# Router products made inside the second out stage instead of at the start of the route block

## The chip, the cores and the metric

The kernel runs on one core of a Trainium2 chip, as one program that is launched once. The metric is the device time of that launch in microseconds (us). The core has a matrix engine (TensorE, in the trace PE, with PEld for its weight loads), a vector engine (VectorE, DVE), a scalar engine (ScalarE, ACT), GpSimd (POOL), a sync engine that here only issues DMAs (SyncE, SP), and 16 DMA engines that all queues share. Each compute engine runs its own list of instructions in order, and they wait for each other by semaphores.

## The reference, cut to what matters

The network is two blocks for 512 tokens of width 1024. The first has two layers: a retention and gated-linear-attention mixer with a dense feed-forward part, then a gated mixer ("hgrn") with a mixture of experts. The second block has attention and a layer of many tiny experts. The change touches the seam between the second mixer and the mixture of experts:

```python
h = h + hgrn2_mixer(hn, lb, c_w_in[e], hgrn_norm_g[e], c_w_out[e])
h = h + moe_swiglu(rms_norm(h, norm_ffn_g[l]), moe_router[e], moe_w_gate[e], moe_w_up[e], moe_w_down[e])

def moe_swiglu(h, w_router, ...):
    logits = (xt @ w_router).astype(jnp.float32)        # 512 tokens x 8 experts
    top_logits, top_idx = lax.top_k(logits, TOP_K)      # TOP_K = 2
    gates = jax.nn.softmax(top_logits, axis=-1)
    ...                                                 # tokens sorted by expert, gate, up and down products
    out = jnp.einsum('nk,nkd->nd', gates.astype(y.dtype), y)
```

## The kernel before, in words

The 512 tokens are four tiles of 128 (`TT` = 4), the width is eight slices of 128 (`KD` = 8). `h` holds the running activations with tokens on partitions, `xT` the normalised input of the next product with the width on partitions. Both stay in SBUF. PSUM is eight banks, `ps[0]` to `ps[7]`.

The program is a row of blocks. A block gives each engine its list; all engines meet at its end, and nothing of the next block begins earlier. Within a block the order on each engine is as the code is written.

The second out stage (`out_stage` with the name "out1", L930) takes the mixer's output and, by token tile, scales heads, transposes (`turn`, L1058), multiplies by `c_w_out` (`project`, L1069), adds to `h` (`join`, L1026), normalises (ACT, L985 to L989, into `mix`), transposes the normalised rows (`turn_norm`, L1079) and writes them into `xT` with the gain (`place`, L1037). SP first loads `w_out`, then stores each normalised tile to `xn_rows` in DRAM, from which the experts gather later, and waits until the four stores have landed. The tail of the stage is tile 3: PE does the projection, `turn_norm(2)`, then `turn_norm(3)`, and DVE places.

The route block (`route_stage`, L1397) comes next. In it SP loads the router weights (32 KB); PE multiplies, in four tiles of eight slices (L1440), `xT` by them; DVE copies the four results (L1470), takes the two largest of eight (L1473, L1476) and marks them in `both`; PE counts, with ones and triangular matrices, how many tokens come before each in its expert (L1447, L1450); DVE works out from that the row of every token (L1495 to L1547). POOL, from the start of the block, sets a row of zeros and a 128x1024 tile of zeros (L1552, L1553), clears the table `token_of_row` (L1555), and when the rows are known scatters the token numbers into it with eight indirect DMAs (L1560). ACT, when the tile of zeros is set, issues one DMA that fills all of `y_rows`, 3072 rows of 4 KB, with zeros (L1457), later does one exponential (L1460), and at its end waits for the fill to land. POOL's last act is to wait for the scatters to land. A float32 product is two passes in the trace, so 32 products are 64 records.

The experts block starts with DVE's memset (L1812), POOL's fetch of indices (L1602) and SP's weight loads.

Of the kernel before, what the change touches and what calls it, by code (L numbers as in the profile page):

```python
# [14 lines left out]
F32 = mybir.dt.float32  # L15
# [7 lines left out]
P = 128  # L23
# [906 lines left out]

def out_stage(S, name, mix, gate, head_gain, w_sb, w, gain, scratch, ahead=None, xn_dram=None):
    nc, h, ps, xT = S.nc, S.h, S.ps, S.xT
    NH, ident = D // P, S.const("ident")
    squares, own, inverse, roots, ready, turned, taken = (
# [12 lines left out]
    with ExitStack() as st:  # L949
        ss = S.sb(name + "_ss", [P, TT, NH], F32, st)  # L950
        r = S.sb(name + "_r", [P, TT, NH], F32, st)
        hs = S.sb(name + "_hs", [P, TT], F32, st)
        hr = S.sb(name + "_hr", [P, TT], F32, st)
        with nc.Block(name) as block:
            @block.sync
            def _(sp):
                for c in range(2):
                    sp.dma_start(w_sb[:, c, :, :], w[:, c * 512:(c + 1) * 512].rearrange("(k p) n -> p k n", p=P)).then_inc(loaded[c].sem, 16)
                if ahead is not None:
                    ahead(sp)  # L960
                if xn_dram is not None:
                    for t in range(TT):
                        sp.wait_ge(h_normed.sem, h_normed.at(t + 1))
                        sp.dma_start(xn_dram[tile(t), :], mix[:, t, :]).then_inc(stored.sem, 16)
                    sp.wait_ge(stored.sem, stored.at(16 * TT))
# [36 lines left out]
            @block.vector  # L1002
            def _(dve):
                nonlocal n_own
                o = Count(own)
                ho = Count(h_own)

                def scale_heads(t):
                    m = mix[:, t, :].rearrange("p (h w) -> p h w", h=NH)
                    dve.wait_ge(squares.sem, squares.at(t + 1))  # L1010
                    nc.vector.tensor_reduce(ss[:, t, :], scratch[:, t % 2, :].rearrange("p (h w) -> p h w", h=NH), AX.X,
                                            ALU.add).then_inc(own.sem, o.up())
                    dve.wait_ge(own.sem, o.value())
                    nc.vector.tensor_scalar(ss[:, t, :], ss[:, t, :], 1.0 / P, EPS, ALU.mult, ALU.add).then_inc(own.sem, o.up())
                    dve.wait_ge(own.sem, o.value())
                    nc.vector.reciprocal(ss[:, t, :], ss[:, t, :]).then_inc(inverse.sem, 1)
                    nc.vector.tensor_tensor(mix[:, t, :], mix[:, t, :], gate[:, t, :], ALU.mult).then_inc(own.sem, o.up())
                    dve.wait_ge(own.sem, o.value())
                    dve.wait_ge(roots.sem, roots.at(t + 1))
                    nc.vector.tensor_tensor(m, m, r[:, t, :].unsqueeze(2).broadcast_to([P, NH, P]), ALU.mult).then_inc(ready.sem, 1)  # L1020

                def join(t):
                    for c in range(2):
                        dve.wait_ge(summed.sem, summed.at(2 * t + c + 1))
                        dst = h[:, t, c * 512:(c + 1) * 512]
# [14 lines left out]

                for t in range(TT):
                    scale_heads(t)
                for t in range(TT):
                    join(t)
                    invert(t)
                    if t:
                        place(t - 1)
                place(TT - 1)
                n_own = o.n

            @block.tensor
            def _(pe):
# [33 lines left out]
                for t in range(2, TT):  # L1086
                    turn(t)
                    turn_norm(t - 2)
                    project(t)
                turn_norm(TT - 2)  # L1090
                turn_norm(TT - 1)
        for sig, n in ((squares, TT), (own, n_own), (inverse, TT), (roots, TT), (ready, TT), (turned, TT), (taken, TT),
                       (h_squares, TT), (h_own, TT), (h_inverse, TT), (h_roots, TT), (h_normed, TT), (h_turned, 2 * TT),
                       (h_placed, 2 * TT), (stored, 16 * TT * (xn_dram is not None)), (loaded[0], 16), (loaded[1], 16),
                       (summed, 2 * TT), (joined, 2 * TT)):
            sig.base += n


def ffn_stage(S, M, mix, gate):
# [248 lines left out]
            s.base += n  # L1348


def mixer1(S, xn_rows):

    a = S.a
    w = a["c_w_in"][0]
    with ExitStack() as st:
# [3 lines left out]
        with ExitStack() as st2:  # L1359
# [9 lines left out]
            with ExitStack() as st3:  # L1369
# [5 lines left out]
            gated_stage(S, "hgrn", 8, 1, lambda p: q[:, p, :], lambda p: keys[:, p, :], lambda p: z[:, p, :],  # L1375
                        lambda hd, c: v[:, c, hd * P:(hd + 1) * P],
                        lambda hd: mix[:, :, hd * P:(hd + 1) * P], 0)
        w_out = S.sb("w_out1", [P, 2, KD, BANK], F32, st)
        scratch = S.sb("out1_squares", [P, 2, D], F32, st)
        out_stage(S, "out1", mix, gate, (S.head_gain["hgrn"], S.head_gain["hgrn"]), w_out, a["c_w_out"][0], S.gains[:, 3, :], scratch,  # L1380
                  xn_dram=xn_rows)


def scale_stage(S, x, by):
# [12 lines left out]
def route_stage(S, R):  # L1397
    nc, a, ps, xT = S.nc, S.a, S.ps, S.xT
    S_ = S.sig
    got, logits, own, gates_in, gates_e, chosen, placed, zeroed, ids, blanked = (  # L1400
        S_("o_" + x) for x in ("got", "logits", "own", "gates_in", "gates_e", "chosen", "placed", "zeroed", "ids", "blanked"))
    cleared, scattered = S_("o_cleared", pool_dma=True), S_("o_scattered", pool_dma=True)
    n_own = 0
    with ExitStack() as st:
        wr = S.sb("router_w", [P, KD, N_EXP], F32, st)
        lg = S.sb("router_lg", [P, TT, N_EXP], F32, st)
        top = S.sb("router_top", [P, TT, 8], F32, st)
        top_i = S.sb("router_ti", [P, TT, 8], U32, st)
        top_f = S.sb("router_tf", [P, TT, 8], F32, st)
# [17 lines left out]
        zero_rows = S.sb("router_zero", [1, LISTED], I32, st)  # L1427
        blank = S.sb("router_blank", [P, D], F32, st)
        with nc.Block("route") as block:
            @block.sync  # L1430
            def _(sp):
                with nc.allow_non_contiguous_dma(reason="32 KB of router weights"):
                    sp.dma_start(wr[:, :, :], a["moe_router"][0].rearrange("(k p) e -> p k e", p=P)).then_inc(got.sem, 16)

            @block.tensor
            def _(pe):
                pe.wait_ge(got.sem, got.at(16))
                for t in range(TT):
                    for k in range(KD):
                        last = nc.tensor.matmul(ps[t][:, 0:N_EXP], xT[:, k, t * P:(t + 1) * P], wr[:, k, :],  # L1440
                                                start=(k == 0), stop=(k == KD - 1))
                    last.then_inc(logits.sem, 1)

                pe.wait_ge(chosen.sem, chosen.at(1))
                for t in range(TT):
                    for u in range(t + 1):
# [17 lines left out]
            def _(dve):  # L1464
                nonlocal n_own
                o = Count(own)
                iota8 = S.const("iota16")[:, 0:8]
                for t in range(TT):
                    dve.wait_ge(logits.sem, logits.at(t + 1))
                    nc.vector.tensor_copy(lg[:, t, :], ps[t][:, 0:N_EXP]).then_inc(own.sem, o.up())  # L1470
                dve.wait_ge(own.sem, o.value())
                for t in range(TT):
                    nc.vector.max(top[:, t, :], lg[:, t, :]).then_inc(own.sem, o.up())  # L1473
                dve.wait_ge(own.sem, o.value())
# [76 lines left out]
            def _(pool):  # L1551
# [9 lines left out]
                            out=R.token_of_row, out_offset=bass.IndirectOffsetOnAxis(ap=R.row[:, t, c:c + 1], axis=0),  # L1561
                            in_=token_i[:, t:t + 1], in_offset=None).then_inc(scattered.sem, 16)
                pool.wait_ge(scattered.sem, scattered.at(16 * 2 * TT))
        for s, n in ((got, 16), (logits, TT), (own, n_own), (gates_in, 1), (gates_e, 1), (chosen, 1), (placed, 1),
                     (zeroed, 2), (cleared, 16), (blanked, 16), (scattered, 32 * TT), (ids, 2)):
            s.base += n

# [295 lines left out]
    return eng.value_load(tile, min_val=lo, max_val=hi)  # L1863


def moe1(S, xn_rows):

    nc, a = S.nc, S.a
    with ExitStack() as st:
# [2 lines left out]
        R.row = S.sb("row_of", [P, TT, 2], I32, st)  # L1872
        R.expert = S.sb("expert_of", [P, 2, 16], I32, st)
        R.units = S.sb("n_units", [P, 2], I32, st)
        R.xn = xn_rows
        R.y = nc.dram_tensor("y_rows", (ROWS_MAX, D), F32, kind="Internal").ap()
        R.token_of_row = nc.dram_tensor("token_of_row", (LISTED, 1), I32, kind="Internal").ap()
        route_stage(S, R)
# [1311 lines left out]
def run_stages(S, out):  # L3190
# [6 lines left out]
    M = modulation(S, S.stack)  # L3197
    xn_rows = S.nc.dram_tensor("xn_rows", (T, D), F32, kind="Internal").ap()
    mixer0(S, M)
    mixer1(S, xn_rows)  # L3200
    for prefix in ("t_", "h_", "q_", "s_", "m_"):
        S.retire(prefix)
    moe1(S, xn_rows)
    row_norm_stage(S, "final1", S.a["final_norm_g"])
    with ExitStack() as st:
        mix = S.sb("mix2", [P, TT, D], F32, st)
# [53 lines left out]
```

## Time and profile before

| what | value |
|---|---|
| time, median of 3 runs | 4557.43 us (4549.16, 4557.43, 4559.23) |
| time of the profiled execution | 4559.06 us |
| span of its trace | 4557.0 us, 2.06 us less than its time |
| PE busy | 3855.7 us, 85% of the span |
| DVE, ACT, POOL busy | 1715.8, 585.3, 1099.9 us |
| mean granted clock of TensorE | 0.907 of full |
| out stage of the second mixer | 1285.8 to 1366.5 us |
| route block | 1366.5 to 1411.8 us |

Times in the trace are microseconds from the start of the span. The chain that ended last, as the page prints it, covers less than one per cent of the span, since the chain breaks at the ends of blocks; so the seam is read from the timeline, from the waits and from the DMA rows.

### The profile page before, as it was taken

Reading aid. Unit: us, or ns where it says so; the run is one execution under the profiler, and the core shown is the slowest. Engines: PE = TensorE matmul, PEld = TensorE weight load, DVE = VectorE, ACT = ScalarE, POOL = GpSimd, SP = SyncE. Lnnn points to the kernel's source line nnn. Section 1 sums busy time; section 2 is a strip of 40 time slices with the busy share of each in tenths; the row PEclk is TensorE's granted clock in tenths of the full one; section 3 lists DMA queues with packets and bytes.
Section 4 is the critical chain, followed back from the end, with each engine's and each line's share of the span. In section 5 each row is a group of like instructions: output and inputs, shape, how many; then the busy total and the mean of one; then the engine's idle time right before and its main releaser. Section 6 shows DMA issues by size and latency. Waiting matters only on the chain. (4 is left out here: it accounts for less than half of the span.)

```text
span 4557.0 us, 45375 instructions
## 1 busy us (share of the span) xinstructions
PE 3855.7 (85%) x17173; PEld 2566.8 (56%) x17180; DVE 1715.8 (38%) x3657; ACT 585.3 (13%) x1486; POOL 1099.9 (24%) x1165
## 2 busy tenths in 40 slices
PE   7988999999676999999999986998666777676666
PEld 3465777644645888888999983465322223222222
DVE  2042231111941000000000004184988776777655
ACT  1121000112320000000000001143111111111111
POOL 0010000000411000000000000000477777777775
PEclk9969999999897999999999998979788888888888
DMA  3103674320017888888777752102799999999998
GB/s 117 56 2 132 235 264 162 138 74 19 1 56 286 298 301 303 307 304 298 257 260 249 259 197 67 54 1 80 298 406 404 420 417 412 420 416 415 418 415 337
DMA packets 531782, 1088.29 MB, mean 239 GB/s; under 512 B 36993, under 2 KB 315934, under 8 KB 531526
## 3 DMA queue, kind: packets, MB, share of 16 engines
q1 hardware_dynamic: 376330, 522.81, 33.5%
q0 software_dynamic: 150976, 546.79, 29.8%
q10 hardware_dynamic: 4348, 17.07, 0.9%
q8 instruction: 69, 1.13, 0.1%
q14 instruction: 59, 0.48, 0.0%
HBM read 1065.29 MB, written 21.28 MB: 238 GB/s over the span
## 5 line engine op out<-in xcount | busy, mean ns | idle before, releaser
L2634 PE MATMUL banks<-peer_ring,mix 128*128 128x512 f32 x1512 | 843.2, 718 | 359.6 <-DMA peer_ring<-in_peer_v_dram,peer_expert 359.6
L2634 PEld LDWEIGHTS banks<-peer_ring,mix 128*128 128x128 f32 x1512 | 337.8, 231 | 861.3 <-DMA peer_ring<-in_peer_v_dram,peer_expert 452.2
L2902 DVE SCALAR_TENSOR_TENSOR peer_ring<-peer_ring,banks 128x1024 f32<-128x1024 f32 x512 | 593.6, 1217 | 250.1 <-DMA peer_ring<-in_peer_u_dram,peer_expert 249.1
L2502 POOL DMA_INDIRECT peer_ring<-in_peer_u_dram,peer_expert x512 | 481.3, 940 | 658.8 <-DVE peer_expert L2836 456.2
L2502 POOL DMA_INDIRECT peer_ring<-in_peer_v_dram,peer_expert x512 | 488.1, 953 | 162.1 <-issue 143.7
L1809 DVE TENSOR_TENSOR experts_hid<-experts_gs,banks 128x128 f32<-128x128 f32 (+1 forms) x224 | 66.5, 297 | 1169.4 <-ACT experts_gs L1781 1169.4
L1690 PEld LDWEIGHTS banks<-rows_xt,experts_wg 128*128 128x128 f32 x3584 | 447.6, 192 | 36.9 <-issue 36.6
L1690 PE MATMUL banks<-rows_xt,experts_wg 128*128 128x128 f32 (+1 forms) x3584 | 463.1, 283 | 3.2 <-DVE rows_xt L1629 3.2
L1690 PE MATMUL banks<-rows_xt,experts_wu 128*128 128x128 f32 (+1 forms) x3584 | 461.8, 282 | 0.0
L1690 PEld LDWEIGHTS banks<-rows_xt,experts_wu 128*128 128x128 f32 x3584 | 441.8, 192 | 0.0
L402 PE MATMUL banks<-xT,proj_w 128*128 128x512 f32 (+2 forms) x736 | 328.1, 604 | 8.7 <-PEq L216 7.1
L1602 POOL DMA_DIRECT2D rows_index<-token_of_row x14 | 8.0, 574 | 1070.6 <-PE banks L1618 1063.1
L405 PE MATMUL banks<-proj_w,xT 128*128 128x512 f32 (+2 forms) x704 | 265.6, 536 | 0.0
L854 POOL TENSOR_TENSOR hgrn_both<-k,hgrn_diff 128x256 f32<-128x256 f32 x56 | 50.6, 910 | 836.5 <-ACT hgrn_diff L799 810.5
L1707 PE MATMUL banks<-experts_wd,experts_hid 128*128 128x512 f32 x560 | 251.9, 592 | 0.0
L402 PEld LDWEIGHTS banks<-xT,proj_w 128*128 128x128 f32 (+2 forms) x736 | 138.0, 189 | 192.2 <-issue 191.4
L1781 ACT ACTIVATE experts_gs<-banks 128x128 f32<-128x128 f32 (+1 forms) x224 | 63.8, 285 | 1174.1 <-PE banks L1690 1174.1
L405 PEld LDWEIGHTS banks<-proj_w,xT 128*128 128x128 f32 x704 | 126.9, 195 | 140.6 <-issue 140.4
L2935 DVE SCALAR_TENSOR_TENSOR banks<-peer_ring,peer_wgt,banks 128x1024 f32<-128x1024 f32 x130 | 167.4, 1288 | 84.6 <-DMA peer_ring<-in_peer_v_dram,peer_expert 83.9
L1720 PE MATMUL banks<-experts_hid,experts_wd 128*128 128x152 f32 x1344 | 180.5, 293 | 0.0
L1720 PEld LDWEIGHTS banks<-experts_hid,experts_wd 128*128 128x128 f32 x1344 | 176.3, 190 | 0.4
L1173 PE MATMUL banks<-xT,ffn_wg 128*128 128x256 f32 x704 | 162.1, 384 | 1.2 <-ACT ada_c L1211 1.2
(449 smaller groups left out, 3635.1 us busy)
## 6 DMA issues: line engine op xcount, KB each, us to landing
experts_wg<-in_moe_w_gate_dram SPq DMA_DIRECT2D x112, 1024.0 KB, 5.1
experts_wu<-in_moe_w_up_dram SPq DMA_DIRECT2D x112, 1024.0 KB, 7.7
experts_wd<-in_moe_w_down_dram SPq DMA_DIRECT2D x112, 1024.0 KB, 8.1
ada_w<-in_w_ada_dram SPq DMA_DIRECT2D x12, 2048.0 KB, 8.0
ffn_wg<-in_ffn_w_gate_dram SPq DMA_DIRECT2D x22, 1024.0 KB, 7.9
ffn_wu<-in_ffn_w_up_dram SPq DMA_DIRECT2D x22, 1024.0 KB, 10.4
ffn_wd<-in_ffn_w_down_dram SPq DMA_DIRECT2D x22, 1024.0 KB, 11.9
proj_w<-in_c_w_in_dram SPq DMA_DIRECT2D x8, 2048.0 KB, 8.5
```

What stands on the lines that cost most here:

```text
L402: last = nc.tensor.matmul(out_of(g), wk[:, m * P:m * P + width], xT[:, k, :], start=(k == 0), stop=(k == KD - 1))
L405: last = nc.tensor.matmul(out_of(g), xT[:, k, m * P:(m + 1) * P], wk[:, 0:n], start=(k == 0), stop=(k == KD - 1))
L1173: last = nc.tensor.matmul(ps[bank][:, 0:ROWS], w[:, b, k, j * P:(j + 1) * P], xT[:, k, u * ROWS:(u + 1) * ROWS], start=(k == 0), stop=(k = ...
L1690: ins = nc.tensor.matmul(ps[bank][:, 0:E.rows], w[:, b, k, j * P:(j + 1) * P], E.xu[:, k, :], start=(k == 0), stop=(k == KD - 1))
L1707: ins = nc.tensor.matmul(ps[hf][:, :], hid[:, j, 0:P], wd[:, b, j, hf * 512:(hf + 1) * 512], start=(first and j == 0), stop=(final and j = ...
L1720: ins = nc.tensor.matmul(ps[d // 2][:, at:at + B.rows], wd[:, b, j, d * P:(d + 1) * P], hid[:, j, :], start=False, stop=False, skip_group_ ...
L1781: nc.scalar.activation(gs[:, j, 0:E.rows], ps[4 + j][:, 0:E.rows], ACT.Silu).then_inc(E.gated[j].sem, 1)
L1809: nc.vector.tensor_tensor(hid[:, j, 0:E.rows], gs[:, j, 0:E.rows], ps[6 + j][:, 0:E.rows], ALU.mult).then_inc(E.hidden[j].sem, 1)
L2502: pool.indirect_dma_start(out=ring[:, slot_of(kind, n, b), :], out_offset=None, in_=tables[kind == "value"], in_offset=bass.IndirectOffset ...
L2634: last = nc.tensor.matmul(ps[bank + hf][:, :], diag[:, n % 2 * B + b, :], ring[:, slot_of("value", n, b), hf * 512:(hf + 1) * 512], start= ...
L2902: nc.vector.scalar_tensor_tensor(row, row, 1.0, rows_at, ALU.mult, ALU.mult, accum_out=acts[:, t % 2, at:at + 1]).then_inc(dotted[q].sem, 1)
L2935: ins = nc.vector.scalar_tensor_tensor(sum_at, row, weight(n, b), sum_at, ALU.mult, ALU.add)
```

## The change

The router weights are loaded by SP in the out stage, after `w_out` and ahead of the stores. PE makes the products there: `route(0)` and `route(1)` between the transposes of tile 2 and those of tile 3, `route(2)` and `route(3)` after them, all into one bank, `ps[0]`, 8 columns a tile. DVE copies the 128x32 result once, after its last `place`, into a tile `router_logits` that lives to the end of the program. The route block loses its SP list, its 32 products and four copies. The semaphores with the prefix `t_` are given free a little earlier, so that the new signals find two.

```diff
+                if logits_to is not None:
+                    with nc.allow_non_contiguous_dma(reason="32 KB of router weights"):
+                        sp.dma_start(router[:, :, :], S.a["moe_router"][0].rearrange("(k p) e -> p k e", p=P)).then_inc(router_got.sem, 16)
                 if xn_dram is not None:
...
                 place(TT - 1)
+                if logits_to is not None:
+                    dve.wait_ge(logits.sem, logits.at(TT))
+                    nc.vector.tensor_copy(logits_to, ps[0][:, 0:TT * N_EXP].rearrange("p (t e) -> p t e", t=TT)).then_inc(own.sem, o.up())
...
+                def route(t):
+                    if logits_to is None:
+                        return
+                    pe.wait_ge(h_placed.sem, h_placed.at(2 * t + 2))
+                    if t == 0:
+                        pe.wait_ge(router_got.sem, router_got.at(16))
+                    for k in range(KD):
+                        last = nc.tensor.matmul(ps[0][:, t * N_EXP:(t + 1) * N_EXP], xT[:, k, tile(t)], router[:, k, :],
+                                                start=(k == 0), stop=(k == KD - 1))
+                    last.then_inc(logits.sem, 1)
+
                 turn_norm(TT - 2)
+                route(0)
+                route(1)
                 turn_norm(TT - 1)
+                route(2)
+                route(3)
...
-            @block.sync
-            def _(sp):
-                with nc.allow_non_contiguous_dma(reason="32 KB of router weights"):
-                    sp.dma_start(wr[:, :, :], a["moe_router"][0].rearrange("(k p) e -> p k e", p=P)).then_inc(got.sem, 16)
-
             @block.tensor
             def _(pe):
-                pe.wait_ge(got.sem, got.at(16))
-                for t in range(TT):
-                    for k in range(KD):
-                        last = nc.tensor.matmul(ps[t][:, 0:N_EXP], xT[:, k, t * P:(t + 1) * P], wr[:, k, :],
-                                                start=(k == 0), stop=(k == KD - 1))
-                    last.then_inc(logits.sem, 1)
-
                 pe.wait_ge(chosen.sem, chosen.at(1))
...
-                for t in range(TT):
-                    dve.wait_ge(logits.sem, logits.at(t + 1))
-                    nc.vector.tensor_copy(lg[:, t, :], ps[t][:, 0:N_EXP]).then_inc(own.sem, o.up())
-                dve.wait_ge(own.sem, o.value())
```

The list of PE at the seam, before: the last projection, both transposes together, the end of the out stage, and the route block with the products and the two counts.

```order
L1069 MATMUL banks<-w_out,xT 128x512 x16
L1079 MATMUL banks<-consts,mix 128x128 x16
L954 UNCONDITIONAL_BRANCH
L1435 UNCONDITIONAL_BRANCH
L1440 MATMUL banks<-router_w,xT 128x8 x32
L1447 MATMUL banks<-router_both,consts 128x8 x10
L1450 MATMUL banks<-router_both,consts 128x8 x4
```

The same place in the changed kernel (its line numbers are higher by 9 to 15):

```order
L1078 MATMUL banks<-w_out,xT 128x512 x16
L1088 MATMUL banks<-consts,mix 128x128 x8
L1106 MATMUL banks<-router_w,xT 128x8 x16
L1088 MATMUL banks<-consts,mix 128x128 x8
L1106 MATMUL banks<-router_w,xT 128x8 x16
L957 UNCONDITIONAL_BRANCH
L1457 UNCONDITIONAL_BRANCH
L1462 MATMUL banks<-router_both,consts 128x8 x10
L1465 MATMUL banks<-router_both,consts 128x8 x4
```

Half of the products now stand ahead of the last transposes, half behind them, and all ahead of the branch that ends the out stage; the counts are the first thing that PE does in the route block. On DVE, before, the four copies open the route block:

```order
L1037 TENSOR_TENSOR xT<-banks,columns 128x4x128 x4
L954 UNCONDITIONAL_BRANCH
L1463 UNCONDITIONAL_BRANCH
L1470 COPY router_lg<-banks 128x8 x4
L1473 MAX router_top<-router_lg 128x8 x4
```

and in the changed kernel one copy closes the out stage:

```order
L1043 TENSOR_TENSOR xT<-banks,columns 128x4x128 x4
L1057 COPY router_logits<-banks 128x32
L957 UNCONDITIONAL_BRANCH
L1478 UNCONDITIONAL_BRANCH
L1484 MAX router_top<-router_logits 128x8 x4
```

The choice of experts is now the first thing that DVE does in the route block. ACT's and POOL's lists at the seam are the same in both.

## Rows read from the trace of the kernel before

**Rows 1.** Page, first line: the span.

```profile
span 4557.0 us, 45375 instructions
```

**Rows 2.** Timeline, tail of out1: start us, us, engine, line, operation, count, idle before.

```profile
1334.83 8.75 PE L1069 MATMUL banks<-w_out,xT 128*128 128x512 f32 x20
...
1359.64 1.04 PE L1079 MATMUL banks<-consts,mix 128*128 128x128 f32 x8
...
1363.57 1.09 PE L1079 MATMUL banks<-consts,mix 128*128 128x128 f32 x8 [2.89 <-ACT mix L989]
1364.26 1.29 DVE L1037 TENSOR_TENSOR xT<-banks,columns 128x512 f32<-128x512 f32 x2 [0.98 <-PE banks L1079]
```

**Rows 3.** Waits of SP's queue, 1340 to 1430: us in total, times, longest.

```profile
SPq L1429 <- PEq L1429: 44.6, 1, 44.6
...
SPq L954 <- DMA xn_rows<-mix: 2.3, 1, 2.3
```

**Rows 4.** Timeline of the route block, 1366 to 1414.

```profile
1366.55 0.39 SPq L1433 DMA_DIRECT2D router_w<-in_moe_router_dram  x1
1366.56 2.86 POOL L1552 MEMSET router_zero<- 1x3328 int32 x1 [86.93 <-POOLq L954]
...
1368.77 13.82 PE L1440 MATMUL banks<-router_w,xT 128*128 128x8 f32 x64 [4.11 <-DMA router_w<-in_moe_router_dram]
1369.36 0.94 POOL L1553 MEMSET router_blank<- 128x1024 f32 x1
1370.34 0.45 ACTq L1457 DMA_DIRECT2D y_rows<-router_blank  x1
1370.62 0.72 POOL L1555 DMA_DIRECT2D token_of_row<-router_zero  x1 [0.31 <-POOL router_blank L1553]
...
1382.63 0.17 DVE L1470 COPY router_lg<-banks 128x8 f32<-128x8 f32 x1 [3.25 <-PE banks L1440]
1382.84 0.37 DVE L1473 MAX8 router_top<-router_lg 128x8 f32<-128x8 f32 x4
...
1384.71 4.43 PE L1447 MATMUL banks<-router_both,consts 128*128 128x8 f32 x20 [2.11 <-DVE router_both L1485]
...
1395.16 0.16 DVE L1534 CAST router_token<-consts 128x4 int32<-128x4 f32 x1
...
1396.24 1.07 POOL L1560 DMA_INDIRECT token_of_row<-router_token,row_of  x1 [24.90 <-DVE router_token L1534]
...
1405.19 0.95 POOL L1560 DMA_INDIRECT token_of_row<-router_token,row_of  x1 [0.31 <-issue]
1411.85 0.27 DVE L1812 MEMSET experts_zero<- 128x256 uint32 x1 [15.09 <-PEq L1429]
```

**Rows 5.** DMA issues, 1340 to 1440: KB each, median us from issue to landing.

```profile
y_rows<-router_blank ACTq DMA_DIRECT2D x1, 12288.0 KB, 39.2
...
token_of_row<-router_token,row_of POOLq DMA_INDIRECT x8, 6.4
...
token_of_row<-router_zero POOLq DMA_DIRECT2D x1, 13.0 KB, 7.8
```

**Rows 6.** Windows, DMA in the route block: us, busy by engine, PEclk, DMA share, GB/s.

```profile
1375.40:1376.50 1.10, 1.10 (x7) 1.10 (x7) 0.17 (x1) 0.00 (x0) 0.00 (x0) 0.50 1.05 403
1376.50:1380.00 3.50, 3.50 (x18) 3.50 (x18) 0.17 (x1) 0.00 (x0) 0.00 (x0) 0.50 1.02 415
1380.00:1396.20 16.20, 8.74 (x41) 8.55 (x40) 7.04 (x54) 0.20 (x1) 0.00 (x0) 0.50 1.02 421
1396.20:1401.20 5.00, 0.00 (x0) 0.00 (x0) 0.48 (x4) 0.00 (x0) 3.95 (x4) 0.50 1.02 422
1401.20:1402.70 1.50, 0.00 (x0) 0.00 (x0) 0.00 (x0) 0.00 (x0) 0.99 (x2) 0.50 0.30 56
1402.70:1411.50 8.80, 0.00 (x0) 0.00 (x0) 0.00 (x0) 0.00 (x0) 2.83 (x3) 0.50 0.03 2
```

**Rows 7.** Windows at the seam, for the granted clock (PEclk).

```profile
1363.50:1364.70 1.20, 1.09 (x8) 0.85 (x8) 0.44 (x1) 0.01 (x1) 0.00 (x0) 1.00 0.32 126
1364.70:1368.70 4.00, 0.00 (x0) 0.00 (x0) 0.85 (x2) 0.00 (x0) 2.14 (x1) 0.52 0.37 101
```

**Rows 8.** Windows at a stretch of 128x1 products in the first block.

```profile
882.40:886.90 4.50, 4.50 (x42) 4.46 (x40) 0.76 (x2) 0.00 (x0) 0.00 (x0) 1.00 0.00 0
887.00:891.90 4.90, 4.90 (x24) 4.86 (x23) 0.00 (x0) 0.00 (x0) 0.00 (x0) 0.50 0.02 3
```

**Rows 9.** Timeline, the change of blocks from hgrn to out1.

```profile
1284.94 0.60 ACT L812 ACTIVATE mix<-banks 128x512 f32<-128x512 f32 x1 [7.62 <-PE banks L911]
1285.79 0.99 SPq L958 DMA_DIRECT2D w_out<-in_c_w_out_dram  x2
```

More of the change, by code:

```diff
@@ L929, in gated_stage, with out_stage @@
             s.base += n
-def out_stage(S, name, mix, gate, head_gain, w_sb, w, gain, scratch, ahead=None, xn_dram=None):
+def out_stage(S, name, mix, gate, head_gain, w_sb, w, gain, scratch, ahead=None, xn_dram=None, logits_to=None):
     nc, h, ps, xT = S.nc, S.h, S.ps, S.xT
@@ L953, in out_stage @@
         hr = S.sb(name + "_hr", [P, TT], F32, st)
+        if logits_to is not None:
+            router = S.sb("router_w", [P, KD, N_EXP], F32, st)
+            router_got, logits = S.sig("o_got"), S.sig("o_logits")
         with nc.Block(name) as block:
@@ L1048, in _ @@
                 place(TT - 1)
+                if logits_to is not None:
+                    dve.wait_ge(logits.sem, logits.at(TT))
+                    nc.vector.tensor_copy(logits_to, ps[0][:, 0:TT * N_EXP].rearrange("p (t e) -> p t e", t=TT)).then_inc(own.sem, o.up())
                 n_own = o.n
@@ L1096, in out_stage @@
             sig.base += n
+        if logits_to is not None:
+            router_got.base += 16
+            logits.base += TT
 def ffn_stage(S, M, mix, gate):
@@ L1348, in close, with mixer1 @@
             s.base += n
-def mixer1(S, xn_rows):
+def mixer1(S, xn_rows, logits):
     a = S.a
@@ L1377, in mixer1 @@
                         lambda hd: mix[:, :, hd * P:(hd + 1) * P], 0)
+        S.retire("t_")
         w_out = S.sb("w_out1", [P, 2, KD, BANK], F32, st)
@@ L1380, in mixer1 @@
         out_stage(S, "out1", mix, gate, (S.head_gain["hgrn"], S.head_gain["hgrn"]), w_out, a["c_w_out"][0], S.gains[:, 3, :], scratch,
-                  xn_dram=xn_rows)
+                  xn_dram=xn_rows, logits_to=logits[:, :, :])
 def scale_stage(S, x, by):
@@ L1399, in route_stage @@
     S_ = S.sig
-    got, logits, own, gates_in, gates_e, chosen, placed, zeroed, ids, blanked = (
-        S_("o_" + x) for x in ("got", "logits", "own", "gates_in", "gates_e", "chosen", "placed", "zeroed", "ids", "blanked"))
+    own, gates_in, gates_e, chosen, placed, zeroed, ids, blanked = (
+        S_("o_" + x) for x in ("own", "gates_in", "gates_e", "chosen", "placed", "zeroed", "ids", "blanked"))
     cleared, scattered = S_("o_cleared", pool_dma=True), S_("o_scattered", pool_dma=True)
@@ L1404, in route_stage @@
     with ExitStack() as st:
-        wr = S.sb("router_w", [P, KD, N_EXP], F32, st)
-        lg = S.sb("router_lg", [P, TT, N_EXP], F32, st)
+        lg = R.logits
         top = S.sb("router_top", [P, TT, 8], F32, st)
@@ L1563, in _ @@
                 pool.wait_ge(scattered.sem, scattered.at(16 * 2 * TT))
-        for s, n in ((got, 16), (logits, TT), (own, n_own), (gates_in, 1), (gates_e, 1), (chosen, 1), (placed, 1),
+        for s, n in ((own, n_own), (gates_in, 1), (gates_e, 1), (chosen, 1), (placed, 1),
                      (zeroed, 2), (cleared, 16), (blanked, 16), (scattered, 32 * TT), (ids, 2)):
@@ L1863, in expert_values, with moe1 @@
     return eng.value_load(tile, min_val=lo, max_val=hi)
-def moe1(S, xn_rows):
+def moe1(S, xn_rows, logits):
     nc, a = S.nc, S.a
@@ L1874, in moe1 @@
         R.units = S.sb("n_units", [P, 2], I32, st)
-        R.xn = xn_rows
+        R.xn, R.logits = xn_rows, logits
         R.y = nc.dram_tensor("y_rows", (ROWS_MAX, D), F32, kind="Internal").ap()
@@ L3199, in run_stages @@
     mixer0(S, M)
-    mixer1(S, xn_rows)
+    logits = S.sb("router_logits", [P, TT, N_EXP])
+    mixer1(S, xn_rows, logits)
     for prefix in ("t_", "h_", "q_", "s_", "m_"):
         S.retire(prefix)
-    moe1(S, xn_rows)
+    moe1(S, xn_rows, logits)
     row_norm_stage(S, "final1", S.a["final_norm_g"])
```

## The prediction, written before the changed kernel ran

> **What bounds the kernel now.** I took the span first [rows 1]: the profiled execution took 4559.06 us, of which 4557.0 are the span and 2.06 lie around it. The change lies in some 50 us of that, so shares of the whole span say nothing; I read the timeline of the seam, then who waits for whom at the ends of the two blocks, then the DMA rows.
>
> In the route block the reader is to see two chains side by side, and that all engines meet at its end: SP, with nothing to do after one DMA, waits 44.6 us for that [rows 3]. The block runs from 1366.55 to 1411.85, 45.3 us [rows 4]. Chain one is the obvious one: weights land, 64 passes of L1440 (13.82 us), the last copy at 1382.63, MAX8 at 1382.84, counts on PE at 1384.71, rows known at 1395.16, eight scatters issued from 1396.24 to 1405.19, the last of them landing. With the median landing of 6.4 us [rows 5] that is 1405.19 + 6.4 = 1411.6, 0.25 before the next block: this chain ends the block now. Chain two starts at the block's start too and uses none of these engines but POOL for two memsets: the tile of zeros, then at 1370.34 the fill of `y_rows`, 12288 KB, landing 39.2 us later, at 1409.5 [rows 4, 5]. It ends only 2.1 us before chain one. The DMA engines are full with it (421 GB/s, share 1.02) until 1401.2 [rows 6]; 12.58 MB at 421 GB/s is 29.9 us, so it can't be much shorter. From 1401.2 to 1409.5 there is a tail in which only some 0.1 MB moves (56 GB/s for 1.5 us, then 2), while the last scatters are issued.
>
> **The change, part by part.** Everything is counted against the profiled execution.
>
> *What goes.* DVE's MAX8 stood 1382.84 - 1366.55 = 16.3 us into the block. It will stand some 0.1 us into it, so chain one moves forward by 16.2 us against the block's start: the first scatter 29.7 - 16.2 = 13.5 us in, the last 38.6 - 16.2 = 22.4 us in, landed at 22.4 + 6.4 = 28.8 us. The one thing that could hold the first scatter is the clearing of the table, issued 4.07 us in and landed 7.8 later, at 11.9 [rows 4, 5]: 1.6 us to spare. ACT's exponential can't come before POOL's memsets and the fill's issue are through, at 4.2 us, but DVE then waits for the counts (until 8 us) anyway.
>
> *What is late next.* The fill. Its start hangs on the memsets at the block's start, which don't move within the block: DMA full until 34.65 us in (1401.2), the small remainder until 36.15 (1402.7) [rows 6]. That is later than 28.8, so from here on chain two decides. What the tail does then is what no row shows. Below: it goes with the scatters that are gone by then, and the block ends at 34.65 + 0.3 = 35.0. Above: it stays as it is, 1409.5 is 42.95 us in, plus 0.3, 43.3. I take the nearer row, the end of the remainder, 36.15. On top come the eight scatters, which now run beside the fill. The nearest row is the clearing: while its packets pass, 403 instead of 421 GB/s for 1.1 us, and 415 in the 3.5 us after [rows 6], 0.05 and 0.05 us; eight such are 0.8 us. From landing to the next block's first instruction 0.3 (at another change of blocks ACT ends at 1285.54 and SP issues at 1285.79 [rows 9]), and 0.4 for the last packet to land. Block: 36.15 + 0.8 + 0.4 + 0.3 = 37.65 instead of 45.3, a gain of 7.65 us. More than half of the 16.2 is thus not to be had.
>
> *What comes.* PE's tail of the out stage [rows 2]. `turn_norm(2)` ends at 1360.68 and PE waits for ACT until 1363.57, 2.89 us. `route(0)` and `route(1)` are 32 passes there. A pass with few columns costs at full clock what 128x1 passes cost: 42 in 4.50 us, 0.107 [rows 8]; 32 are 3.42 us, to 1364.10, so `turn_norm(3)` is 0.53 late and ends at 1365.2. Then `route(2)` and `route(3)`, 32 passes, for which the clock decides. It is granted at 1.00 (2.4 GHz) until about 1364.8, then 0.50 (1.2 GHz) [rows 7]. Before it fell PE had done one burst of eight transposes after 2.89 us of nothing. The new passes fill the time, but passes of few columns did not keep or win the clock in this trace: it fell at 886.9 in the middle of an unbroken run of them [rows 8], and 13.82 us of L1440 ran at 0.50 to the end [rows 4, 6]. So I price them at half clock: 13.82/64 = 0.216 each, 6.9 us, to 1372.1. If the clock stayed, they'd cost 3.4; if it fell before `route(0)`, the first 32 would cost 3.4 more and the transposes 0.9 more. The copy adds 0.1 wait and 0.2: 1372.4. `place(3)` is through by 1366.5 and is hidden. Before, the stage ended with SP's wait for the last store [rows 3] at about 1366.2; that store doesn't move and is now hidden too. With 0.25 for the change of blocks the route block starts at 1372.65 instead of 1366.55: 6.1 us later. All that the block holds, the fill first, starts later by that. The 32 KB of weights come behind 4 MB of `w_out`, some 60 us before they are wanted, and SP's first store comes 30 us later: no cost.
>
> **The sum.** +6.1 - 7.65 = -1.55 us. All that follows shifts as a whole. By bounds: best +2.7 (full clock) - 10.3 = -7.6; worst +10.4 (clock lost early) - 2.0 = +8.4. The profiled execution lies 1.6 above the median of the runs, so a run like it would take 4557.5, and 4556 to 4557 is what I expect of a median; I say 4556.5.
>
> **Rivals.** *A, the fill is held up by the scatters in its midst (the other side: slower).* Between 1402.7 and 1409.5 the rest of the fill crept, in the very stretch where POOL issued one scatter every 1.27 us. If an engine gives the fill a packet only as each scatter passes, then eight scatters inside the fill hold such an engine for 8 x 1.27 = 10.2 us, and the block ends at 36.15 + 10.2 + 0.7 = 47.05: +1.75 and +6.1, +7.9 us in all, 4566. It decides from 7.65 - 6.1 = 1.55 us of hold-up. Against it: four scatters were issued from 1396.2 to 1401.2 and the rate stayed at 422 GB/s [rows 6], and the clearing cost little. The Trainium skill ("DMA: Bandwidth & Descriptors", section on latency and other measured facts) calls two of the 16 engines usually slower, with contention by GpSimd's descriptor rings as a guess; by that the tail belongs to one or two engines and stays whole, which is the upper bound of 43.3 above, +4.1 us in all. No row splits the engines. Chance 0.2 for A and this weaker form together.
>
> *B, the scatters don't get through until the fill has.* The first was issued at 1396.24 and the fill filled the engines until 1401.2; with 6.4 us to landing it landed after the fill's end. If they queue, all eight land in a burst behind 34.65 us, in 6.4 us at least and 10.4 (1401.2 to 1411.6) at most: block 41.4 to 45.4, taken 42.5, so +3.3 us, 4561. Against it: the clearing, issued at 1370.62 into the same load, landed in 7.8 us [rows 5], long before the fill's end. The same page (section on queues, rings and completion order) says that a DMA engine takes turns between its queues; by that rule B is out, and the clearing's row agrees. Chance 0.12.
>
> *C, the fill doesn't bound the block, and the chain's 16.2 us count in full.* 6.1 - 16.2 = -10.1, 4548. For it: nothing but the tail's obscurity; 12.58 MB would have to go at over 500 GB/s. Chance 0.05.
>
> *D, the clock stays at 1.00 through `route(2)` and `route(3)`.* 3.5 us less than forecast, -5.0, 4553. For it: PE is never idle now from 1334 to the end of the stage. Against: rows 8. Chance 0.08.
>
> **How the numbers follow.** Forecast 0.55, A 0.2, B 0.12, C 0.05, D 0.08. What a measurement can tell from no change is 0.2%, about 9 us; the three runs shown alone lie 10 us apart. The forecast, B and D are inside it wholly, A nearly (+7.9), C just outside. With the runs' own scatter: faster 0.1, same 0.8, slower 0.1. The range goes from 4549 (C's edge and the lowest run) to 4564 (most of A).
>
> **What would show it.** PE's L1106 in two groups of 32 records, the second near 0.21 us a record; the first in the hole before the last transposes; route block starting near 1372.7; MAX8 at once; first scatter some 13.5 us after its start; the block 37 to 38 us long, and its end at the landing of the fill, not of the scatters. It is wrong if the block is under 33 us (C) or over 41 (A, B), or the second group runs at 0.107 (D). A change elsewhere in the trace of more than a few us would be a cause that I haven't seen.

## The result, and the profile after

The changed kernel is slower: 1.0074 times the kernel before, 95% interval 1.0061 to 1.0086, medians 4591.65 us (five runs) and 4559.23 us (seven). Measured again beside the kernel before (run e1_after) it was 1.0088 (1.0071 to 1.0105), medians 4596.55 and 4557.19. Forecast was 4556.5, no change. Two more runs of the changed kernel were disturbed (6398 us at a mean granted clock of 0.587, and 17699 us) and are left out, and the trace read here is that of e1_after.

```profile
span 4588.3 us, 45433 instructions
```

The span is 31.3 us above the one before [rows 1]. The first look goes to the seam. From the timeline of e1_after, the tail of out1, in the form of [rows 2]; L1088 is `turn_norm`, L1106 the router products, L1043 `place`, L1057 the new copy:

```profile
1349.99 1.04 PE L1088 MATMUL banks<-consts,mix 128*128 128x128 f32 x8
1350.86 3.64 PE L1106 MATMUL banks<-router_w,xT 128*128 128x8 f32 x32
...
1354.36 1.38 PE L1088 MATMUL banks<-consts,mix 128*128 128x128 f32 x8
1355.03 1.44 DVE L1043 TENSOR_TENSOR xT<-banks,columns 128x512 f32<-128x512 f32 x2 [1.39 <-PE banks L1088]
1355.53 6.83 PE L1106 MATMUL banks<-router_w,xT 128*128 128x8 f32 x32
1362.40 0.19 DVE L1057 COPY router_logits<-banks 128x32 f32<-128x32 f32 x1 [5.94 <-PE banks L1106]
1362.88 2.86 POOL L1563 MEMSET router_zero<- 1x3328 int32 x1 [92.66 <-POOLq L957]
```

The first 32 passes take 3.64 us and lie in the old hole, the second 32 take 6.83, the copy follows at once. The granted clock in the same three stretches (PEclk is the third value from the end):

```profile
1349.90:1354.30 4.40, 4.40 (x41) 4.31 (x40) 2.19 (x5) 2.50 (x4) 0.00 (x0) 1.00 0.00 0
1354.30:1355.50 1.20, 1.20 (x10) 1.20 (x10) 0.47 (x1) 0.00 (x0) 0.00 (x0) 0.78 0.67 266
1355.50:1362.40 6.90, 6.87 (x34) 6.77 (x32) 0.91 (x2) 0.00 (x0) 0.00 (x0) 0.50 0.09 32
```

PE was busy throughout, and the clock still fell to 0.50 (1.2 GHz) at about 1355, as in [rows 7, 8]. From the transposes of tile 2 to POOL's first memset it is 12.89 us now, 6.92 before (1359.64 to 1366.56): +5.97.

The route block, in the form of [rows 4]:

```profile
1362.91 0.37 DVE L1484 MAX8 router_top<-router_logits 128x8 f32<-128x8 f32 x4 [0.32 <-PEq L957]
...
1364.00 1.78 DVE L1490 CAST router_tf<-router_ti 128x32 f32<-128x32 uint32 x1
...
1366.69 0.45 ACTq L1472 DMA_DIRECT2D y_rows<-router_blank  x1
...
1377.92 1.07 POOL L1571 DMA_INDIRECT token_of_row<-router_token,row_of  x1 [10.22 <-DVE router_token L1545]
...
1386.88 0.96 POOL L1571 DMA_INDIRECT token_of_row<-router_token,row_of  x1 [0.30 <-issue]
1411.64 0.27 DVE L1823 MEMSET experts_zero<- 128x256 uint32 x1 [33.21 <-PEq L1456]
```

MAX8, the choice of the experts, comes at once, the eight scatters are issued from 15.0 to 24.0 us into the block, and then there are 24 us in which no compute engine does anything. The block is 48.76 us long, 3.5 us longer than the 45.29 of before. Its DMA issues, in the form of [rows 5], and the DMA in windows, in the form of [rows 6]:

```profile
y_rows<-router_blank ACTq DMA_DIRECT2D x1, 12288.0 KB, 44.4
token_of_row<-router_token,row_of POOLq DMA_INDIRECT x8, 13.0
```

```profile
1368.00:1383.50 15.50, 4.53 (x22) 4.43 (x21) 5.73 (x39) 0.67 (x2) 4.36 (x5) 0.50 1.02 420
1383.50:1388.00 4.50, 0.00 (x0) 0.00 (x0) 0.00 (x0) 0.00 (x0) 3.42 (x4) 0.50 1.19 249
1388.00:1398.00 10.00, 0.00 (x0) 0.00 (x0) 0.00 (x0) 0.00 (x0) 0.00 (x0) 0.50 1.03 167
1398.00:1402.50 4.50, 0.00 (x0) 0.00 (x0) 0.00 (x0) 0.00 (x0) 0.00 (x0) 0.50 1.09 88
1402.50:1410.00 7.50, 0.00 (x0) 0.00 (x0) 0.00 (x0) 0.00 (x0) 0.00 (x0) 0.50 0.91 367
```

The DMA rate is 420 GB/s, falls to 249, 167 and 88 GB/s while the DMA engines stay fully busy (share 1.03 to 1.19; it can exceed 1, since the times of packets are added up), and recovers as the last scatter lands (issued at 1386.88, landed 16.8 us later, at 1403.7). The queues in the slow stretch, 1383.5 to 1402.5: packets, MB, and the time of their packets as a share of the 16 engines' time; q10 is the fill, q0 the scatters:

```profile
q10 hardware_dynamic: 777, 3.18, 105.1%
q0 software_dynamic: 256, 0.00, 2.9%
```

In the full stretch before it, 1368 to 1383.5, q10 has

```profile
q10 hardware_dynamic: 1585, 6.49, 101.9%
```

So the scatters hardly take time of the engines themselves. A packet of the fill takes 16 x 15.5 x 1.019 / 1585 = 0.16 us in the full stretch and 16 x 19 x 1.051 / 777 = 0.41 us beside the scatters, on average. The fill lands 44.4 us after its issue, at 1411.1, and the next block begins 0.5 later. So the seam costs 5.97 + 3.47 = +9.4 us. That leaves most of the loss to be found elsewhere, and the forecast had nothing elsewhere.

It is in the last block, whose 1024 gathers (L2513, L2502 before) bring table rows of 4 KB into `peer_ring`. `peer_ring` is their ring of buffers. For that tile the trace answers with first and last issue (behind the durations in ns); before, then e1_after:

```profile
L2502 POOL DMA_INDIRECT peer_ring<-in_peer_u_dram,peer_expert x512: 933/937/1421, 3189.1 to 4487.4; - x171
L2502 POOL DMA_INDIRECT peer_ring<-in_peer_v_dram,peer_expert x512: 932/937/1919, 3313.7 to 4522.3; - x171
```

```profile
L2513 POOL DMA_INDIRECT peer_ring<-in_peer_u_dram,peer_expert x512: 932/937/1810, 3192.8 to 4517.2; - x171
L2513 POOL DMA_INDIRECT peer_ring<-in_peer_v_dram,peer_expert x512: 932/937/1935, 3317.4 to 4552.6; - x171
```

3189.1 to 4522.3 is 1333.2 us, 3192.8 to 4552.6 is 1359.8: +26.6. A window of 1000 us in this stage, before and in e1_after:

```profile
3500.00:4500.00 1000.00, 701.71 (x1301) 282.59 (x1302) 698.92 (x1367) 115.20 (x378) 751.94 (x796) 0.85 1.02 417
```

```profile
3500.00:4500.00 1000.00, 696.93 (x1272) 281.47 (x1273) 684.74 (x1344) 113.02 (x371) 733.22 (x777) 0.84 1.02 407
```

417 against 407 GB/s with the DMA share at 1.02 in both: the stage is bound by DMA, and the same engines, equally busy, move 2.4% less. The gathers' queue in this window, before and in e1_after:

```profile
q0 software_dynamic: 114384, 416.52, 102.3%
```

```profile
q0 software_dynamic: 111720, 406.81, 102.3%
```

Fewer packets in the same engine time: each takes 2.4% longer. What reads the ring is not slower (median of L2902, now L2913, on VectorE 1217 ns in both, of the products on PE 592 ns in both). No instruction of this stage was changed. What was changed is where its tiles lie: `router_logits`, 128 bytes on each partition, is allocated for the rest of the program, and all tiles allocated after it begin 128 bytes higher. `peer_ring` went from address 153088 (a multiple of 256, and of 512) to 153216 (128 above one), as the allocations add up.

The two parts are 9.4 + 26.6 = 36.0 us; the ratios, at 4557 us, say 33.7 (27.8 to 39.2) and 40.1 (32.4 to 47.8). The spans of the two traces differ by 31.3 only. The rest is in stretches that the change leaves alone and that differ from one execution to the next: up to `turn_norm(2)` e1_after took 9.65 us less than before (in e2_pad128 below, where nothing before the seam differs in its instructions either, the fill was issued 9.2 us earlier), and between the combination of the experts' results and the first gather into `peer_ring` 4.8 us more. So single traces are compared here stage by stage, and the whole by the ratios.

### The profile page after: what moved, and what is told of

Its sections match the earlier page's. It is cut to its first block and busy times, and to the rows that moved or that the text cites. A ratio compares the mean times of both kernels' runs of the same rounds, so it can differ in the third digit from the quotient of the medians.

```text
span 6396.5 us, 45433 instructions
## 1 busy us (share of the span) xinstructions
PE 5914.2 (92%) x17173; PEld 3431.9 (54%) x17180; DVE 1715.0 (27%) x3654; ACT 585.7 (9%) x1486; POOL 1097.7 (17%) x1165
## 5 line engine op out<-in xcount | busy, mean ns | idle before, releaser
L2645 PE MATMUL banks<-peer_ring,mix 128*128 128x512 f32 x1512 | 1068.6, 885 | 182.1 <-DMA peer_ring<-in_peer_v_dram,peer_expert 182.1
L1701 PEld LDWEIGHTS banks<-rows_xt,experts_wg 128*128 128x128 f32 x3584 | 707.1, 260 | 86.1 <-issue 77.7
L1701 PE MATMUL banks<-rows_xt,experts_wg 128*128 128x128 f32 (+1 forms) x3584 | 738.9, 387 | 2.4 <-DVE rows_xt L1640 2.4
L1701 PE MATMUL banks<-rows_xt,experts_wu 128*128 128x128 f32 (+1 forms) x3584 | 738.6, 387 | 0.0
L1701 PEld LDWEIGHTS banks<-rows_xt,experts_wu 128*128 128x128 f32 x3584 | 705.8, 269 | 6.6
L2913 DVE SCALAR_TENSOR_TENSOR peer_ring<-peer_ring,banks 128x1024 f32<-128x1024 f32 x512 | 593.7, 1218 | 263.6 <-DMA peer_ring<-in_peer_u_dram,peer_expert 262.7
L2513 POOL DMA_INDIRECT peer_ring<-in_peer_u_dram,peer_expert x512 | 483.1, 943 | 804.2 <-DVE peer_expert L2847 570.6
L402 PE MATMUL banks<-xT,proj_w 128*128 128x512 f32 (+2 forms) x736 | 542.9, 926 | 7.6 <-PEq L216 6.6
L2513 POOL DMA_INDIRECT peer_ring<-in_peer_v_dram,peer_expert x512 | 491.2, 959 | 193.8 <-issue 127.3
L405 PE MATMUL banks<-proj_w,xT 128*128 128x512 f32 (+2 forms) x704 | 460.6, 842 | 0.0
L1718 PE MATMUL banks<-experts_wd,experts_hid 128*128 128x512 f32 x560 | 444.1, 966 | 0.0
L1200 PE MATMUL banks<-xT,ffn_wu 128*128 128x256 f32 x704 | 279.3, 583 | 0.0
L1210 PE MATMUL banks<-ffn_wd,ffn_hid 128*128 128x512 f32 x352 | 274.9, 967 | 0.0
```

The lines of the kernel that those rows point to most:

```text
L402: last = nc.tensor.matmul(out_of(g), wk[:, m * P:m * P + width], xT[:, k, :], start=(k == 0), stop=(k == KD - 1))
L405: last = nc.tensor.matmul(out_of(g), xT[:, k, m * P:(m + 1) * P], wk[:, 0:n], start=(k == 0), stop=(k == KD - 1))
L1200: last = nc.tensor.matmul(ps[bank][:, 0:ROWS], w[:, b, k, j * P:(j + 1) * P], xT[:, k, u * ROWS:(u + 1) * ROWS], start=(k == 0), stop=(k = ...
L1210: last = nc.tensor.matmul(ps[2 * s + half][:, :], hid[:, j, s * P:(s + 1) * P], wd[:, b, j, half * 512:(half + 1) * 512], start=(g == 0 an ...
L1701: ins = nc.tensor.matmul(ps[bank][:, 0:E.rows], w[:, b, k, j * P:(j + 1) * P], E.xu[:, k, :], start=(k == 0), stop=(k == KD - 1))
L1718: ins = nc.tensor.matmul(ps[hf][:, :], hid[:, j, 0:P], wd[:, b, j, hf * 512:(hf + 1) * 512], start=(first and j == 0), stop=(final and j = ...
```

## The experiments

**The changed kernel again, and the kernel before with its tiles moved.** e1_after is the changed kernel.

> The changed kernel again, for a trace at the usual clock and for its time beside the kernel before. Theory 1 (placement): the new tile router_logits, 128 bytes a partition, lives to the end of the program and moves every later tile by 128 bytes, so that the ring into which the last block gathers its table rows (peer_ring) no longer begins on a multiple of 256 bytes; then the route block is at most 5 us off the forecast, and the 1240 us of gathers take some 30 us longer (about 410 GB/s instead of 420), whole +30 to +37 us. Theory 2 (seam): the scatters hold up the fill or the clock is lost at the seam; then the surplus of some 33 us stands between 1360 us and the experts' first product, and the gathers run at 420 GB/s. Theory 3 (experts): their weight loads are slower, surplus between 1430 and 2720 us.

Measured: 1.0088, with the trace above. Theory 1 holds for the larger part and theory 2 for a smaller one: the gathers took 26.6 us longer, and the route block was not within 5 us of the forecast, as theory 1 alone would have it, but 11 us longer (48.76 against 37.65). The experts' stage, from its first memset to the first gather of the combination, took 1310.6 us against 1311.4, so theory 3 falls.

e2_pad128 is the kernel before with one more line:

```diff
+    S.sb("unused", [P, TT, N_EXP])
     mixer1(S, xn_rows)
```

> The kernel before with nothing but an unused tile of 128 bytes a partition allocated where the changed kernel has router_logits; no instruction differs but in SBUF addresses. Theory 1 (placement): +30 to +35 us, in the gathers of the last block. Theories 2 and 3 as far as they need the moved instructions: within 0.1% of the kernel before.

Measured: 1.0053 (1.0037 to 1.0070), +24 us. Its gathers:

```profile
L2502 POOL DMA_INDIRECT peer_ring<-in_peer_u_dram,peer_expert x512: 932/937/1813, 3179.7 to 4503.5; - x171
L2502 POOL DMA_INDIRECT peer_ring<-in_peer_v_dram,peer_expert x512: 932/937/1937, 3304.4 to 4540.1; - x171
```

1360.4 us. An unused tile of 128 bytes, with every instruction of before, brings the whole +27 in the gathers. The whole is less than the +30 to +35 expected.

**The changed kernel with its tiles put back.** e3_after_512:

```diff
-    logits = S.sb("router_logits", [P, TT, N_EXP])
+    logits = S.sb("router_logits", [P, 4 * TT, N_EXP])[:, 0:TT, :]
```

> The changed kernel with router_logits allocated four times as large (512 bytes a partition, of which the first 128 are used), so that every later tile moves by 512 bytes in all and keeps its place modulo 512. Theory 1 (placement): the surplus goes, and what is left is the seam's own effect, -2 us by the forecast, within -8 to +8. Theory 2: stays at +30 us.

Measured: 1.0014 (1.0004 to 1.0024), +6.4 us. The gathers go from 3196.7 to 4530.9, 1334.2 us, as before. What is left is the seam: route block from 1369.78 to 1418.80, 49.0 us, fill landing after 44.6. By the ratio it is +1.8 to +10.9 us, by the trace +9.4.

e4_after_ring:

```diff
+        S.sb("peer_gap", [P, 96], F32, st)
         ring = S.sb("peer_ring", [P, 2 * B, D], F32, st)
```

> The changed kernel with an unused tile of 384 bytes a partition just ahead of peer_ring, so that the ring and what lies behind it in the last stage are back on their place modulo 512, and the experts' and the attention's tiles stay moved by 128. Theory 1, if the ring alone is it: the whole surplus of 30 us goes, as in the run with the 512-byte tile. If the experts' weight loads have a share (theory 3): that share stays.

Measured: 1.0014 (1.0005 to 1.0024), gathers 1333.7 us. The same as with all tiles put back, so moving the experts' and the attention's tiles by 128 bytes cost nothing to be seen. That is no test of alignment in those stages: by the allocations their large tiles lay off a multiple of 256 before as well (the experts' first weight tile at 76992, 192 above one, and now at 77120, 64 above one). What aligning them would give, no run shows.

**Which tile and which step.** Four kernels are the kernel before with unused bytes ahead of and behind `peer_ring` (e8_behind128 has none ahead and 128 behind):

```diff
+        S.sb("gap_ahead", [P, 16], F32, st)          # 16, 32 or 64 words: 64, 128 or 256 bytes
         ring = S.sb("peer_ring", [P, 2 * B, D], F32, st)
+        S.sb("gap_behind", [P, 112], F32, st)        # so that both make 512
```

> The kernel before with unused tiles of 64 bytes ahead of peer_ring and 448 behind it: the ring alone moves by 64 bytes, its neighbours by 512. If it is the ring's place modulo 256 that sets the gathers' rate: gathers 1333 -> about 1360 us, +25 us in all. If only a shift by 128 hurts, or another tile is the cause: no change.

> The kernel before with the ring alone moved by 128 bytes (128 ahead, 384 behind). Theory 1, the ring's place: +25 us, as in the run in which all tiles moved by 128 (+24). If another tile of the last stage than the ring is the cause: no change.

> The kernel before with the ring alone moved by 256 bytes (256 ahead, 256 behind). If a multiple of 256 is what counts: within 0.1% of the kernel before. If a multiple of 512 is needed, or any shift against the neighbours costs: +12 to +25 us.

> The kernel before with 128 unused bytes behind peer_ring: the ring stays, the weights, sums and keys behind it move by 128. Theory 1: no change, within 0.1%. If VectorE's operands behind the ring are the cause: +25 us.

| ring moved by | behind it moved by | ratio (95%) | gathers, first to last issue | 3500 to 4500 |
|---|---|---|---|---|
| 64 bytes | 512 | 1.0064 (1.0047 to 1.0080) | 3189.5 to 4550.4, 1360.9 us | 407 GB/s |
| 128 | 512 | 1.0063 (1.0045 to 1.0081) | 3179.9 to 4541.1, 1361.2 us | 407 GB/s |
| 256 | 512 | 0.9998 (0.9989 to 1.0008) | 3185.5 to 4517.6, 1332.1 us | 417 GB/s |
| 0 | 128 | 1.0004 (0.9994 to 1.0014) | 3188.7 to 4522.2, 1333.5 us | 417 GB/s |

It is the ring alone, and a multiple of 256 bytes is enough. 64 and 128 bytes off cost the same within the intervals. The windows of e5_ring64 and e7_ring256:

```profile
3500.00:4500.00 1000.00, 685.82 (x1272) 278.09 (x1274) 685.84 (x1345) 113.21 (x371) 732.86 (x777) 0.84 1.02 407
```

```profile
3500.00:4500.00 1000.00, 707.75 (x1308) 285.14 (x1310) 698.00 (x1366) 116.09 (x385) 752.28 (x796) 0.85 1.02 417
```

The Trainium skill ("DMA: Bandwidth & Descriptors", section on how a descriptor splits into AXI transactions) says that an aligned descriptor goes out in pieces of 256 bytes, and that a read which starts off such a boundary also moves the bytes below it. It speaks of reads; here the side that was moved is the one written, in SBUF. The step at 256 agrees with it. By its count of pieces, an estimate, a row of 4096 bytes goes from 16 to 17 for either shift, 6%, and by its count of bytes a shift of 128 costs twice one of 64; the runs show 2.4% less for both. So the size of the loss comes out of neither count. That extra pieces are the cause is argued; that the address is, is shown.

**What the scatters do to the fill.** e9_after_wait, on top of e3_after_512:

```diff
                 pool.wait_ge(ids.sem, ids.at(2))
+                pool.wait_ge(blanked.sem, blanked.at(16))
                 for t in range(TT):
```

> The changed kernel with router_logits at 512 bytes, and POOL waits for the fill of y_rows to land before it issues the first scatter. If the scatters slow the fill (rival A in another form): the fill goes at 420 GB/s to its end and lands some 33 us after its issue instead of 44.4; then come the eight scatters alone, some 10 us of issuing and 3 to 5 to land, block about 51 us. If the fill is slow for another reason (more bytes, its later start, DMA engines busy otherwise): it still lands after 44 us.

Measured: 1.0025 (1.0015 to 1.0034). Its issues and windows:

```profile
y_rows<-router_blank ACTq DMA_DIRECT2D x1, 12288.0 KB, 32.8
token_of_row<-router_token,row_of POOLq DMA_INDIRECT x8, 3.8
```

```profile
1374.00:1383.50 9.50, 3.95 (x19) 3.85 (x19) 5.41 (x37) 0.11 (x1) 0.00 (x0) 0.50 1.02 405
1383.50:1402.50 19.00, 0.00 (x0) 0.00 (x0) 0.34 (x3) 0.00 (x0) 0.00 (x0) 0.50 1.02 410
```

Without scatters beside it the fill keeps above 400 GB/s and lands after 32.8 us; the scatters then land in 3.8 instead of 13.0 (medians). The block, 1368.30 to 1420.73, is 52.4 us, since one follows the other.

e10_after_half, on top of e3_after_512, has `for t in range(TT // 2)` around the scatters, so that only the tokens of tiles 0 and 1 reach the table; the scatters of the others are left out.

> The changed kernel with router_logits at 512 bytes and only the four scatters of token tiles 0 and 1; those of tiles 2 and 3 are left out, so that the experts work on other rows. If each scatter takes its share from the fill: the fill lands about 38.5 us after its issue, midway between 33 and 44.4, and the route block is some 6 us shorter than with eight. If it is the mere presence of scatters, or something else in the block: still 44.

Measured in one execution: the fill lands after

```profile
y_rows<-router_blank ACTq DMA_DIRECT2D x1, 12288.0 KB, 37.9
```

and the block, 1362.33 to 1404.61, is 42.3 us. So 0, 4 and 8 scatters give 32.8, 37.9 and 44.6 us: 1.3 and 1.7 us for each. Each scatter carries 128 numbers of 4 bytes, 512 bytes in all, next to nothing at 420 GB/s. That the scatters lengthen the fill is shown by this row of three; why a packet of the fill takes longer beside them is not.

**The fill out of the way.** e11_after_early, on top of e3_after_512: POOL sets the zeros in the out stage, SP issues the fill there, and the route block has none.

```diff
+                if fill is not None:
+                    sp.wait_ge(zeroed.sem, zeroed.at(1))
+                    sp.dma_start(fill.rearrange("(a p) d -> p a d", p=P),
+                                 blank[:, :].unsqueeze(1).broadcast_to([P, ROWS_MAX // P, D])).then_inc(blanked.sem, 16)
                 if xn_dram is not None:
...
-                act.dma_start(R.y.rearrange("(a p) d -> p a d", p=P),
-                              blank[:, :].unsqueeze(1).broadcast_to([P, ROWS_MAX // P, D])).then_inc(blanked.sem, 16)
```

> The changed kernel with router_logits at 512 bytes, the tile of zeros set by POOL and the fill issued by SP in the out stage, behind the weights there. The fill (30 us) is over by 1335. Then the route block is chain one alone: first scatter 13 to 15 us in, last issued at 24, landed by 29; 29 to 31 us instead of 48.8, and the whole 17 to 19 us below the run with the 512-byte tile, 8 to 12 us below the kernel before. If chain one is slow by itself when it starts early: 35 us or more.

Measured: 0.9982 (0.9971 to 0.9992), median 4545.0 us, 8 us below the kernel before by the ratio (4 to 13). From the load of `w_out` to the route block it is 86.5 us, as in e3_after_512, so the early fill costs the out stage nothing. The route block of e11_after_early, its first memset, first scatter, last scatter, and on DVE the start of the next block:

```profile
1362.62 2.87 POOL L1575 MEMSET router_zero<- 1x3328 int32 x1 [85.54 <-POOLq L960]
...
1377.69 1.07 POOL L1582 DMA_INDIRECT token_of_row<-router_token,row_of  x1 [11.17 <-DVE router_token L1557]
...
1386.64 0.95 POOL L1582 DMA_INDIRECT token_of_row<-router_token,row_of  x1 [0.30 <-issue]
1392.87 0.27 DVE L1834 MEMSET experts_zero<- 128x256 uint32 x1 [14.66 <-PEq L1472]
```

The block is 30.25 us long, as forecast for chain one alone (29 to 31). e12_before_early does the same to the kernel before.

> The kernel before with the same early fill and the products still in the route block (semaphores with the prefix t_ are given free before the out stage, as in the changed kernel). Chain one decided there already: the block shortens only by the quicker landing of the last scatters, some 2 to 3 us, 4555 us. Against it the early fill of the changed kernel shows what moving the products is worth once the fill is out of the way: -16.2 + 6.1, about -10 us.

Measured: 0.9998 (0.9987 to 1.0009); block from 1354.77 to 1399.68, 44.9 us, only 0.4 shorter where 2 to 3 had been expected, since chain one ends it: the last scatter landed 4.9 us after its issue here and 5.3 before (median of all eight before: 6.4), so there was little to win. In both, 1.35 us lie between that landing and the next block. Between the two, the products moved are worth 44.91 - 30.25 = 14.7 us in the block, less 6.0 in the out stage: 8.7, and by the ratios 0.9998 - 0.9982 = 0.0016, 7 us. e11_after_early is the one version that beats both kernels.

## Why the prediction was wrong

*"All that follows shifts as a whole."* This step failed, and with it the range. The tile `router_logits`, which lives to the end of the program, stood in the text and in the code, and the sum priced it at nothing, without a reason. It moved a buffer of a stage that is bound by DMA for 1333 us, 1800 us further on, off a multiple of 256 bytes: +26.6 us in the trace, +24 and +29 by the ratios of the runs that change no instruction (e2_pad128, e6_ring128). No rival had it. The share of 1.02 with 417 GB/s in that stage could have been read before the run, and the addresses could have been worked out from the allocations; that a buffer 128 bytes off costs there, no row of before showed. Without this part the time lies at the range's upper end, 4564: with the ring put back (e3_after_512) the median was 4565.5, +6.4 us by the ratio, against -1.55 in the sum. What is left of the miss is the next step.

*"Eight such are 0.8 us."* The term for the scatters beside the fill was mis-sized: 44.6 - 32.8 = 11.8 us (e3_after_512, e9_after_wait). The row I took, the clearing of the table, moved 13 KB in pieces of up to 832 bytes; the scatters write 4 bytes at a time. The row nearer in kind was the stretch from 1401.2 on, in which the rest of the fill crept while scatters were issued. That the four scatters issued by 1401.2 left the rate at 422 GB/s did not speak against it: by the queues' rows of before, not one packet of theirs had moved by then,

```profile
DMA packets 515, 2.11 MB, mean 422 GB/s; under 512 B 0, under 2 KB 0, under 8 KB 515
```

from 1396.2 to 1401.2, all of them the fill's 4 KB. In e1_after too none had from 1377.9 (the first issue at 1377.92) to 1382, and the rate falls from 1383.5. An issue was taken for the work that follows some 5 us later. The term closes the seam's account: 11.8 - 0.8 = 11.0 us, and the seam came out at +9.4 where -1.55 was forecast, 10.95.

*Rival A* was therefore nearest to what the seam did, +9.4 against its +7.9, though not by its mechanism: it had an engine wait for each next scatter, and the hold-up lasts in e1_after until 1402.5, some 15 us after the last issue, with packets of the fill under way all the time (105.1%) and each taking longer. So that the two sizes lie close is luck. A had 0.2, the forecast 0.55.

*Right:* chain two decides once chain one is early; the fill ends the block. The clock falls at the same place in spite of a busy PE, and 32 passes cost 6.83 (6.9 forecast) and 3.64 (3.42). The route block starts 5.97 later (6.1). B is out: the scatters pass beside the fill. C is out by 48.8 us. D is out by PEclk 0.50. The first scatter came 15.0 instead of 13.5 us into the block, since a cast on VectorE took 1.6 us longer (see the last section); the fill ends the block, so this adds nothing to it directly. Chain one was read as ending 0.25 us before the next block, with the median landing of 6.4; the last scatter's own was 5.3, and 1.35 us lay behind it. The bare fill was sized well: 32.8 us to landing, where 36.15 - 3.8 + 0.4 = 32.75 had been put.

## What to carry to other kernels

A new tile is also a shift of all tiles behind it: look for the longest stage that is bound by DMA, and put its target buffers on multiples of 256 bytes, by padding if need be, and measure it (here it was one ring for gathers of 4 KB rows). When a chain is taken off the path, ask not only what is late next but whether the two now meet: here the scatters were moved from the fill's end into its middle, and gave back the gain and more. Scattered writes of a few bytes are priced by what they do to a bulk transfer beside them, not by their bytes. When a row is to show that two transfers don't disturb each other, see first that packets of both moved in it.

## What the runs showed of the hardware that was not expected

- Gathers of 4 KB rows into SBUF ran at 417 GB/s into a buffer at a multiple of 256 bytes a partition and at 407 GB/s 64 or 128 bytes off, DMA share 1.02 in both; reads of the same buffers by VectorE and PE kept their durations (1217 and 592 ns).
- Eight indirect DMAs of 128 four-byte writes to DRAM took a fill of 12.58 MB from 420 to between 249 and 88 GB/s for some 19 us, with the DMA share above 1: a 4 KB packet of the fill took 0.41 us on average instead of 0.16. The first packets of the scatters passed some 5 us after the first issue.
- VectorE's cast of 128x32 took 1.78 us (L1490, from 1364.00) where it had taken 0.18 before; it ended when POOL's memset of 2.86 us, begun at 1362.88, did. In e11_after_early it was 1.78 again beside the same memset, in e12_before_early, without a memset beside it, 0.18.
